# Merging waits and moving convolution taps in the attention stretch of a hybrid decoder layer

## The reference

```python
proj = h @ w_in                       # 2048 -> conv inputs, q, three k/v pairs, gates
y_conv = b_gate * conv3(c_gate * c_h) # depthwise, 3 taps, 1024 channels
kc = compress(k_c); vc = compress(v_c)            # 15 compressed keys
o_cmp = softmax(q kc) vc              # 16 heads, head_dim 64, 4 kv heads
o_slc = softmax(q ks) vs              # at 256 tokens all 4 blocks are selected
o_win = softmax(q kw) vw
y_attn = g0 * o_cmp + g1 * o_slc + g2 * o_win
y = concat([rmsnorm(y_conv), rmsnorm(y_attn)]) @ w_out
```

## Time and profile before

| | |
|---|---|
| time, median of 3 runs | 1893.9 us (1893.67 to 1894.39) |
| the profiled execution: its time, its span | 1894.39 us, 1892.6 us |
| busy: PE, DVE, ACT, POOL | 1865.3, 1037.6, 883.1, 252.7 us |
| granted TensorE clock | 0.999 of full speed |
| DMA | 366.72 MB, mean 194 GB/s |

### The profile page before, as it was taken

The page is one execution under the profiler, slowest core; times in us unless marked ns, Lnnn a source line. Parts: engine busy times, 40 slices in busy tenths (PEclk is TensorE's granted clock), DMA queues, the critical chain, the costliest instruction groups (busy, mean ns, idle before and its releaser), DMA issues.

```text
span 1892.6 us, 23078 instructions
## 1 busy us (share of the span) xinstructions
PE 1865.3 (99%) x8387; PEld 1531.8 (81%) x8387; DVE 1037.6 (55%) x1129; ACT 883.1 (47%) x1123; POOL 252.7 (13%) x442
## 2 busy tenths in 40 slices
PE   9999999999999999999998899999999999999998
PEld 7888888888888888888776788888888888888886
DVE  5555555554544444668566766445555555545444
ACT  6444444444444444556555645444444444444443
POOL 1111222111100000000132200111111112200000
PEclk9999999999999999999999999999999999999999
DMA  7666666666655556665433565766666666676564
GB/s 258 209 201 199 200 211 212 210 205 193 213 176 200 200 189 200 195 209 175 146 118 100 171 192 164 220 199 196 210 214 201 204 194 202 211 231 195 194 192 142
DMA packets 199517, 366.72 MB, mean 194 GB/s; under 512 B 19028, under 2 KB 23872, under 8 KB 199328
## 3 DMA queue, kind: packets, MB, share of 16 engines
q1 hardware_dynamic: 185568, 353.41, 59.3%
q0 software_dynamic: 11648, 12.02, 2.2%
q10 hardware_dynamic: 2240, 0.47, 0.1%
HBM read 350.11 MB, written 4.19 MB: 187 GB/s over the span
## 4 chain that ended last, share of the span: by engine, by line
PE 92%; DVE 5%; ACT 3%; issue 1%; ACTq 0%; DVEq 0%
PE ps L586 30%; PE ps L588 30%; PE ps L587 30%; DVE w_lo L1382 2%; PE ps L607 1%; ACT prob L1175 1%; ACT w_hi L977 1%; DVE mins L1627 1%; DVE pT_lo L1633 1%; DVE p_h L1684 0%; PE ps L875 0%; PE ps L636 0%; DVE p_q L1653 0%; PE ps L845 0%; DVE shifted L1650 0%
## 5 line engine op out<-in xcount | busy, mean ns | idle before, releaser
L1382 DVE TENSOR_TENSOR w_lo<-raw,w_hi 128x1024 fp32r<-128x1024 f32 x656 | 798.1, 1229 | 653.3 <-ACT w_hi L977 651.5
L977 ACT ACTIVATE w_hi<-raw 128x1024 fp32r<-128x1024 f32 x656 | 689.8, 1060 | 729.4 <-PE ps L588 720.5
L586 PE MATMUL ps<-w_hi,hT_hi 128*128 128x512 f32 x1760 | 688.0, 391 | 5.2 <-DVE w_lo L1382 5.2
L588 PE MATMUL ps<-w_hi,hT_lo 128*128 128x512 f32 x1760 | 685.4, 389 | 0.0
L587 PE MATMUL ps<-w_lo,hT_hi 128*128 128x512 f32 x1760 | 685.1, 389 | 0.0
L586 PEld LDWEIGHTS ps<-w_hi,hT_hi 128*128 128x128 f32 x1760 | 330.5, 188 | 75.4 <-DVE w_lo L1382 3.9
L588 PEld LDWEIGHTS ps<-w_hi,hT_lo 128*128 128x128 f32 x1760 | 330.3, 188 | 69.5
L587 PEld LDWEIGHTS ps<-w_lo,hT_hi 128*128 128x128 f32 x1760 | 330.5, 188 | 67.6
L528 POOL DMA_DIRECT2D gu_raw<-gu_sq x352 | 187.8, 542 | 854.6 <-DVE gu_sq L1443 778.5
L586 PE MATMUL ps<-w_hi,guT_hi 128*128 128x512 f32 x704 | 274.3, 390 | 0.0
L588 PE MATMUL ps<-w_hi,guT_lo 128*128 128x512 f32 x704 | 274.0, 389 | 0.0
(11 more groups left out here) (212 smaller groups left out, 833.1 us busy)
## 6 DMA issues: line engine op xcount, KB each, us to landing
raw<-in_ffn_wg_dram SPq DMA_DIRECT2D x176, 512.0 KB, 4.4
raw<-in_ffn_wu_dram SPq DMA_DIRECT2D x176, 512.0 KB, 4.7
raw<-in_ffn_wd_dram SPq DMA_DIRECT2D x176, 512.0 KB, 4.0
raw<-in_w_in_dram SPq DMA_DIRECT2D x88, 512.0 KB, 3.6
raw<-in_w_out_dram SPq DMA_DIRECT2D x32, 512.0 KB, 4.7
gu_raw<-gu_sq POOLq DMA_DIRECT2D x352, 32.0 KB, 4.3
x_parked<-x SPq DMA_DIRECT2D x8, 256.0 KB, 5.8
raw<-in_cmp_k_w_dram SPq DMA_DIRECT2D x8, 256.0 KB, 2.9
```

The source lines that it names most:

```text
L586: mm(o, x_hi, w_hi[:, s, kk, :], start=first and kk == 0, stop=False)
L588: ins = mm(o, x_lo, w_hi[:, s, kk, :], start=False, stop=last and kk == GK - 1)
L977: act.activation(w_hi[:, c % SLOTS, :, :], raw[:, c % SLOTS, :, :], ACT.Copy).then_inc(hi_ready, 1)
L1382: tt(w_lo[:, s, :, :], raw[:, s, :, :], w_hi[:, s, :, :].bitcast(F32), ALU.subtract).then_inc(lo_ready, 1)
```

## The change

It touches the order of small pieces of work alone; no arithmetic is added or dropped.

1. `sum_inverse(m)` moves from the end of DVE's list at group 62 + m to group 63 + m, behind `prob_low` and ahead of `score_min(m + 1)`.
2. `conv_tap(n, tap)` at eight groups becomes `conv_taps` (both taps of a pair: four instructions, with a wait for DVE itself after each two) at groups 75, 79, 87, 91, the last entry of DVE's list there.
3. `conv_tap0(n)` joins `u_operand(n)`: ACT does it one group earlier, right behind the copy.
4. `q_high` moves from groups 44, 48, 52, 53 to 32, 34, 40, 42, `q_low` from 45, 49, 54, 55 to 34, 36, 42, 43.
5. The compressed scores of both query tiles are done after group 54, not after 54 and 55.
6. DVE's `conv_gate(2)`, `conv_gate(3)` move from groups 94, 95 to 93, 94; `conv_gate(0)`, `(1)` from 98 to 99; `attended(7)` from 100 to 99. PE transposes `cb` 0 and 1 after group 97, not 96. ACT's `conv_operand(0)` moves from 98 to 99.

```diff
-                put(at(54), lambda: compressed_scores(0))
-                put(at(55), lambda: compressed_scores(1))
+                put(at(54), compressed_scores)
...
-                put(o, lambda: conv_transposes(("cb", 0)), lambda: conv_transposes(("cb", 1)))
+                put(o + 1, lambda: conv_transposes(("cb", 0)), lambda: conv_transposes(("cb", 1)))
...
                 act.activation(uT[:, 2 * n:2 * n + 2, 2:TOK + 2], ps[:, bank, :].rearrange("p (k t) -> p k t", k=2),
                                ACT.Copy).then_inc(free[bank], 1)
-
-            def conv_tap0(n):
-                bank, u = USE["cu", n]
                 act.wait_ge(free[bank], u + 1)
                 for c in (2 * n, 2 * n + 1):
                     act.activation(cv(c), uT[:, c, 0:TOK], ACT.Copy,
...
-                for n, c in enumerate((44, 48, 52, 53)):
+                for n, c in enumerate((32, 34, 40, 42)):
                     put(at(c), lambda n=n: q_high(n))
...
                             put(TICK0 + 2 + m, lambda n=n: u_operand(n))
-                            put(TICK0 + 3 + m, lambda n=n: conv_tap0(n))
...
-                put(o + 2, lambda: conv_operand(0))
-                put(o + 3, lambda: conv_operand(1))
+                put(o + 3, lambda: conv_operand(0), lambda: conv_operand(1))
...
+            def conv_taps(tiles):
+
+                for n in sorted({c // 2 for c in tiles}):
+                    bank, u = USE["cu", n]
+                    dve.wait_ge(free[bank], u + 1)
+                w = lambda tap, c: vecs[:, V_CONVW + tap * CT + c:V_CONVW + tap * CT + c + 1]
+                for tap in (1, 2):
+                    for c in tiles:
+                        if tap == 1:
+                            dve.wait_ge(tap0_ready, (c + 4) % CT + 1)
+                        ins = stt(out=cv(c), in0=uT[:, c, tap:tap + TOK], scalar=w(tap, c), in1=cv(c),
+                                  op0=ALU.mult, op1=ALU.add)
+                    seq(ins)
...
-                for n, c in enumerate((45, 49, 54, 55)):
+                for n, c in enumerate((34, 36, 42, 43)):
                     put(at(c), lambda n=n: q_low(n))
...
+                    if 1 <= m <= NT * HEADS:
+                        put(c, lambda m=m: sum_inverse(m - 1))
                     if m < NT * HEADS:
                         put(c, lambda m=m: score_min(m))
-                    if output_at(m) is not None and output_at(m) < UNITS - 1:
+                    if output_at(m) is not None:
                         put(c, lambda u=output_at(m): attended(u))
...
-                for m in range(NT * HEADS):
-                    put(TICK0 + 2 + m, lambda m=m: sum_inverse(m))
-                for n, slots in ((2, (76, 78)), (3, (80, 81)), (0, (88, 89)), (1, (92, 93))):
-                    for tap in (1, 2):
-                        put(at(slots[tap - 1]), lambda n=n, tap=tap: conv_tap(n, tap))
+                put(at(75), lambda: conv_taps([4, 5]))
+                put(at(79), lambda: conv_taps([6, 7]))
                 put(at(82), conv_input_lower)
+                put(at(87), lambda: conv_taps([0, 1]))
+                put(at(91), lambda: conv_taps([2, 3]))
                 o = OUT0
-                put(o - 2, lambda: conv_gate(2))
-                put(o - 1, lambda: conv_gate(3), lambda: conv_operand(2))
+                put(o - 3, lambda: conv_gate(2))
+                put(o - 2, lambda: conv_gate(3))
+                put(o - 1, lambda: conv_operand(2))
                 put(o, lambda: conv_operand(3))
-                put(o + 2, lambda: conv_gate(0), lambda: conv_gate(1))
-                put(o + 3, lambda: conv_operand(0))
-                put(o + 4, lambda: conv_operand(1), lambda: attended(UNITS - 1))
+                put(o + 3, lambda: conv_gate(0), lambda: conv_gate(1), lambda: conv_operand(0))
+                put(o + 4, lambda: conv_operand(1))
```

More of the change, by code:

```diff
@@ L836, in compressed_kv, with compressed_scores @@
                 ins.then_inc(full[bank], 1)
[L838 to L851, removed]
+            def compressed_scores():
                 bank, u = USE["cs",]
@@ L858, in compressed_masks @@
                    skip_group_check=True)
+                for t in range(NT):
+                    for q in range(HEADS // 2):
+                        ins = mm(ps[:, bank, (t * (HEADS // 2) + q) * 2 * NCP:][:, 0:2 * NCP],
+                                 qT[:, q, t * P:t * P + P], kcT[:, q // GRP, :, :].rearrange("p a n -> p (a n)"),
+                                 start=False, stop=True, skip_group_check=True)
+                ins.then_inc(full[bank], 1)
             def compressed_prob_transposes(t):
```

## The result

The changed kernel takes 1903.96 us (median of 5, 1902.31 to 1905.65) against 1894.39 for the kernel before beside it: +9.6 us, a ratio of 1.0051 with a 95% interval of 1.0036 to 1.0066. Slower, as forecast; 1902.2 had been predicted, from a median of 1893.9 for the kernel before, so +8.3 where +9.6 came. The profiled execution took 1904.49 us with a span of 1902.7, 10.1 over the one before.

A forecast was written before the change was run, and what follows sets the result against it. An ACT-DVE loop bounds the kernel from group 75 on. Terms 7.1 - 1.3 + 3.9 + 0.2 - 0.4 - 1.2 = +8.3 us gave 1902.2 us for the median, range 1895 to 1908.5.

The forecast's parts named there:

- The bound: From group 75 on, a loop between ACT and DVE that doesn't pass through PE sets the pace; additions cost full price.
- DVE's taps: Four taps exposed behind `attended` at groups 75, 79, 87, 91: +1.78 each, +7.1; old places give back 0.8.
- ACT's first tap: Tap between exponentials and `hi` at four groups, from group 73: 0.91 and 0.06 each, +3.9 us.
- The inverses: Reciprocal ahead of `score_min`, +1.1 over 14 groups; POOL's scaling ends before `lo`, -1.5; together -0.4 us.
- The late scaling: PE waits 1.5 to 2.5 us for POOL at groups 73, 77, 81, absorbed: 0. Rival: not absorbed, +6, chance 0.15.
- Queries: Query pieces moved into the half-size groups leave PE's time unchanged: 0, with 1.4 us if one is late.
- The compressed scores: They end a group sooner; PE does the same matmuls and nobody late waits for them: 0.
- The end: Earlier gates reach group 98 2.0 us sooner; later stalls 0.7 and 1.3, less today's 1.2: -1.2 us.

The follow-up runs named there:

- a5_split: The changed kernel with the compressed scores again done after groups 54 and 55: 1903.47 us, 0.5 less than the changed kernel.
- a_taps_off2: The changed kernel with its `conv_taps` one group later, at 76, 80, 88 and 92: 1896.21 us, 7.8 less than the changed kernel.

## Why the prediction was right, and where it was off

- **The bound.** Right. The pace of groups 75 to 97 is the loop of `hi`, `lo`, `prob_low`, `score_min`, `exps`; cutting it took 16.7 us off.
- **DVE's taps, +7.1 and -0.8 at the old places.** The mechanism is right: 1.80 us of taps exposed, 1.82 to 1.84 at each place of the changed kernel, 7.3 together, for the 1.78 forecast. Measured alone +7.2 against +6.3: there each place was 1.84 to 2.01, and the old places gave back 0.4, not 0.8.
- **ACT's first tap, +3.9 (3.7 alone).** Right: the changed kernel's `lo` ends later by 1.05, 1.00, 1.01 and 0.89 at groups 74, 78, 86, 90. That the edit alone also measured +3.9 is partly luck: in its trace the four places make 3.6 and a fall of the clock 0.8.
- **The inverses, -0.4.** With `conv_input_lower` and the taps that no longer wait for the exponentials, -1.4 was reckoned for this edit alone before the waits for POOL were put on: -1.4 was measured. `lo` went from 1303 to 1226 ns, where 1.22 us had been assumed. The minimum beside POOL's scaling took 0.67 us (at 1025.75 us of the changed kernel's trace, with the scaling from 1025.93), as without it. That agrees with the Trainium skill (SBUF — State Buffer, "Who interferes with whom"), which says a reduction doesn't contend with GpSimd.
- **The late scaling, 0.** Right that PE waits and that the loop covers it. What I missed is that waits of this length can bring the clock down.
- **Queries, 0.** Right: +0.2, inside the noise.
- **The compressed scores, 0.** This is the step that failed: "PE does the same matmuls and nobody late waits for them: 0." The matmuls are the same, but in a row they are followed by a stretch at half clock in some executions (seven of eleven of edit 5 alone, by the two heaps of its times), and one stretch cost 1.6 us in both traces that have it. The changed kernel's profiled execution is one of them. That nobody late waits for them was right; what the term left out is the clock behind them.
- **The end, -1.2.** Mis-sized: -0.7. Less was gained ahead of group 98 (1.7, not 2.0) and more given back behind it (1.2, not 0.8).

For the profiled execution the account closes. At group 94 `lo` ended 10.87 us later than before. 1.64 of these were there at group 72, from the clock at group 55, and 9.23 are the loop's, where the sum had 9.5. The end took 0.7 off, not 1.2. Together 1902.7 + 1.6 - 0.3 + 0.5 = 1904.5, and 1904.49 was measured.

The six edits alone add up to -1.4 + 7.2 + 3.9 + 0.2 + 1.6 - 0.7 = +10.8, and together give +9.6. The traces show two pieces of the 1.2 between them: the 0.8 that the clock cost edit 3 alone, and 0.5 by which edit 2's four places were dearer alone (7.8) than in the changed kernel (7.3). Neither piece is in the changed kernel's trace. These are single executions, and no run shows that the same holds for the medians.

## What to carry to other kernels

When a bound engine idles a little in every step, look for a chain of the other engines that goes round once a step without it, and write down its links in order: what stands on it costs full price, what stands beside it is free, and the 13 us of waits beside it were worth 1.4 here. A better place for four cheap instructions is behind the link that leaves the engine idle, not behind one that it reaches last. Best of all is to take a link out of the chain: computing the minimum one step earlier than the weights' remainder gave 16.7 us, where the best reordering of the small pieces (edit 1) gave 1.4.

## What the runs showed of the hardware that was not expected

PE's clock can fall while PE is never idle. At or right behind 32 products of 32 columns in a row it was granted at half (from 891.1 us in the changed kernel, 892.4 in edit 5 alone), and in two other traces with the same products it was not. With another group between the two halves of them it never was in these traces. The stretch cost 1.6 us.

In or behind single waits of PE of 1.9 to 2.9 us it fell too: 2.3 and 2.6 us after groups 73 and 87 of the changed kernel, 1.9 after group 81 in edit 1 alone. It did not at each of them: not at 2.6 and 2.5 us after groups 77 and 91 of the changed kernel, nor at 1.9 after group 77 in edit 1 alone. The kernel before, whose longest wait is 1.8 us, kept the clock up throughout the mixer.

Such a stretch cost nothing on the loop in the changed kernel, and 0.8 us at each of two places in `a5_split`, where it made PE's transposes later than ACT wanted them. Whether it comes differs between executions: the changed kernel and `a_taps_off2` have the same lists up to group 75, and one has the fall at group 55, the other not. That would explain the spread of the runs, 3 to 4 us for the changed kernel and for the edits 3 and 5 alone against 1.7 us for 21 runs of the kernel before, but no run shows it: edit 2 alone, with four falls in its trace, spreads by 0.8.
